# Two x loads of a decoder trunk's start change queue and place, and 18 idle matmuls stand where 14 stood

## The chip, the cores and the metric

One NeuronCore of a Trainium2 chip runs the whole program; the other cores are idle. The time is the device time of one launch in microseconds, the median over several runs. Inputs and weights lie in HBM, all in float32.

## The reference

Two layers of a decoder trunk on 256 tokens of width 2048. Layer 0 mixes with a retention group of four heads and a gated linear recurrence of eight channel blocks, layer 1 with block-sparse attention of sixteen heads; behind each mixer stands a gated MLP with a causal convolution of width 3. What the change touches is the very beginning, the norm and the first projection of layer 0:

```python
def rmsnorm(x, g):
    x32 = x.astype(jnp.float32)
    y = x32 * lax.rsqrt(jnp.mean(x32 * x32, axis=-1, keepdims=True) + EPS)
    return (y * g.astype(jnp.float32)).astype(x.dtype)
...
for l in range(DEPTH):
    hn = rmsnorm(x, norm_mix[l])
    if l % 2 == 0:
        y = even_mixer(hn, ...)      # proj = hn @ w_in, 2048 x 6144
    else:
        y = odd_mixer(hn, ...)
    x = x + y
    x = x + conv_ffn(rmsnorm(x, norm_ffn[l]), ...)
```

## The kernel before

**Layout.** x is held transposed in SBUF as `x_res`, 128 partitions by 16 k tiles by 256 tokens, and all weights stream through once. A matrix product is cut into output blocks of 512 columns (`NB`), and each block into eight chunks of two k tiles (`CT`), so a chunk of W is 256 rows by 512 columns, 512 KB. Chunks pass through a ring of four buffers (`RING`).

**The split.** Every float32 factor is split into a high and a low part of type float32r, which TensorE multiplies in three products. For W, ScalarE rounds `raw` to `w_hi` (line 368) and VectorE subtracts to get `w_lo` (line 942). For x, ScalarE makes `xs[..., 0, :]`, x times the norm's gain, rounded (line 397), and VectorE the remainder (line 991). The row scale of the norm is applied later, when a block is drained. TensorE then does per k tile and 128 output columns one matmul of w_hi with both parts of x (512 columns, line 663) and one of w_lo with the high part (256 columns, line 667); a chunk is eight of each.

**What sets the order.** There is no planner: each engine's program is written out by hand, and semaphores tie them together. Each engine walks the same sequence of chunks:

- SyncE (SP) issues the loads of W: chunk 0 is loaded as two tiles of 256 KB (line 286) with a semaphore of its own each, `tile_landed` and `landed[0]`. Between the following chunks it issues the x loads of k tiles 4 to 15 in three pieces of 512 KB (line 294), and a table of parameters (line 289). From the fifth chunk on, a load waits until VectorE has read the ring buffer (line 276).
- ScalarE issues at its start the gains of the norms (`par`, 32 KB, line 355) and two x loads of 256 KB, k tiles 0 and 1 (line 356, semaphore `first_loaded`) and k tiles 2 and 3 (line 357, `x_loaded[0]`). Then it loads a function table and rounds `ones`. For chunk 0 of the first block it waits for gains and first x load (lines 581 and 582), makes xs of two k tiles, waits for the first W tile, rounds it, waits for the second, rounds it. For chunk 1 it waits for `x_loaded[0]`, makes xs of k tiles 2 and 3, and rounds chunk 1 of W; then it squares the first four k tiles (line 392) for the norm's sum.
- VectorE follows with the low parts and, on odd chunks, sums the squares (lines 1001 to 1014), which end in `sumsq`.
- TensorE begins with `WARM` = 14 matmuls of a matrix of ones (lines 841 to 843), whose result nothing reads. They wait only for the memset of `ones` on GpSimd. Then come the chunks; ahead of chunk 2 stands a small product for the attention's bias, and ahead of chunk 7 the sum of squares over the partitions (line 712), which waits for `sumsq`.

A chunk of TensorE waits for `first_lo` (x's low part) and `lo_ready` (w_lo); in chunk 0 the first k tile waits for `tile_lo` alone.

Of the kernel before, what the change touches and what calls it, by code (L numbers as in the profile page):

```python
# [28 lines left out]
BT = NB // P  # L29
CT = 2  # L30
RING = 4
WARM = 14
KC = KT // CT
FC = FT // CT

# [91 lines left out]
def build(nc, x_t, params, w_gates, rope, decay, rel_bias, buckets, identity,  # L127
# [8 lines left out]
    def place(name, shape, dtype=F32, offset=None):  # L136
        size = int(np.prod(shape[1:])) * 4
        if offset is None:
            offset = at[0]
            at[0] += (size + 31) // 32 * 32  # L140
        return nc.alloc_sbuf_tensor_at(name, shape, dtype, offset=offset), offset
# [4 lines left out]
    x_res, _ = place("x_res", [P, KT, S])  # L146
# [61 lines left out]
    def sem(name):  # L208
        return nc.alloc_semaphore(name)
# [5 lines left out]
    first_loaded, gain_loaded = sem("first_loaded"), sem("gain_loaded")  # L215
    tile_landed, tile_hi, tile_lo, tail_done = sem("tile_landed"), sem("tile_hi"), sem("tile_lo"), sem("tail_done")
    x_loaded = [sem(f"x_loaded{j}") for j in range(4)]
# [50 lines left out]
    @block.sync  # L268
    def _(sp):
        def load(w, q, c, cols, rows):  # L270

            s = c % RING
            turn = q + c // RING
            if not (isinstance(turn, int) and turn == 0):

                sp.wait_ge(lo_ready, RING * (turn - 1) + s + 1)
            src = w[bass.ds(rows * (CT * P), CT * P), cols].rearrange("(t p) n -> p t n", p=P)
            sp.dma_start(raw[:, s, :, :], src).then_inc(landed[s], 16)

        for ph in phases:  # L280
            l = ph.layer
            for b, (_, _, col) in enumerate(ODD_BLOCKS if l else EVEN_BLOCKS):
                for c in range(KC):
                    if (l, b, c) == (0, 0, 0):
                        for u, landing in enumerate((tile_landed, landed[0])):
                            sp.dma_start(raw[:, 0, u, :], w_in[0][u * P:(u + 1) * P, col:col + NB]).then_inc(landing, 16)
                        continue
                    if (l, b, c) == (0, 0, 5):
                        sp.dma_start(par[:, 4 * KT:], params[:, 4 * KT:]).then_inc(const_loaded, 16)
                    load(w_in[l], ph.q_in + 2 * b, c, slice(col, col + NB), c)  # L290
                    if (l, b) == (0, 0) and c in (1, 3, 4):
                        j = (1, 3, 4).index(c) + 1
                        part = slice(j * BT, (j + 1) * BT)
                        sp.dma_start(x_res[:, part, :], x_t[:, part, :]).then_inc(x_loaded[j], 16)
            for b in range(OUTB):
                for c in range(KC):
                    load(w_out[l], ph.q_out + 2 * b, c, slice(b * NB, (b + 1) * NB), MIX_ORDER[l][c])
            with sp.Fori(0, PAIRS) as j:
                for half in range(2):
                    for c in range(KC):  # L300
                        load(w_up[l], ph.q_up + 4 * j + 2 * half, c, bass.ds(j * NB + half * D_FF, NB), c)
            for b in range(OUTB):
                cols = slice(b * NB, (b + 1) * NB)
                for c in DOWN_HEAD:
                    load(w_down[l], ph.q_down, FC * b + c, cols, c)
                with sp.Fori(*DOWN_TURNS) as t:
                    for i in range(RING):
                        load(w_down[l], ph.q_down + t, FC * b + i, cols, RING * t + i)
                for c in DOWN_TAIL:
                    load(w_down[l], ph.q_down, FC * b + c, cols, c)  # L310

        for m in range(BT):

            sp.wait_ge(last_added, m + 1)
            k = KT - BT + m
            sp.dma_start(out_t[:, k, :], x_res[:, k, :]).then_inc(last_stored, 16)
        sp.wait_ge(last_stored, 16 * BT)
# [33 lines left out]
    def _(eng):  # L351
# [1 line left out]
        step = Steps(eng, act_step)  # L353

        eng.dma_start(par[:, 0:4 * KT], params[:, 0:4 * KT]).then_inc(gain_loaded, 16)
        eng.dma_start(x_res[:, 0:CT, :], x_t[:, 0:CT, :]).then_inc(first_loaded, 16)
        eng.dma_start(x_res[:, CT:BT, :], x_t[:, CT:BT, :]).then_inc(x_loaded[0], 16)
        eng.wait_ge(consts_set, 1)
        act_f(ones_r[:, :], ones[:, :], ACT.Copy).then_inc(ones_rounded, 1)

# [33 lines left out]
        def split_x_pair(c):  # L394

            for t in range(CT * c, CT * (c + 1)):
                ins = act_f(xs[:, t, 0, :], x_res[:, t, :], ACT.Copy, scale=param("gain", t))
            ins.then_inc(first_hi, 1)
# [174 lines left out]
        for ph in phases:  # L573
            l = ph.layer
            post = odd_post if l else even_post
            for b in range(INB):
                if (l, b) == (0, 1):
                    eng.wait_ge(const_loaded, 16)
                for c in range(KC):
                    if (l, b, c) == (0, 0, 0):  # L580
                        eng.wait_ge(gain_loaded, 16)
                        eng.wait_ge(first_loaded, 16)
                        split_x_pair(0)
                        eng.wait_ge(tile_landed, 16)
                        act_f(w_hi[:, 0, 0, :], raw[:, 0, 0, :], ACT.Copy).then_inc(tile_hi, 1)
                        eng.wait_ge(landed[0], 16)
                        act_f(w_hi[:, 0, 1, :], raw[:, 0, 1, :], ACT.Copy).then_inc(hi_ready, 1)
                        continue
                    if (l, b) == (0, 0):

                        if c == 1 or c % 2 == 0:
                            eng.wait_ge(x_loaded[c // 2], 16)
                        split_x_pair(c)
                    split(ph.q_in + 2 * b, c)
                    if (l, b) == (0, 0) and c % 2:
                        square_x(c // 2, 0)
                    if b == 0 and l:
                        residual(c, 3, phases[0].n_down + 3, RING * ph.q_in, 1, 2)
                    if (l, b, c) == (0, 0, 5):
                        eng.wait_ge(line_done, 1)  # L600
                        act_f(line[0:HEADS, :], ps[0:HEADS, 5, 0:3 * P], ACT.Copy).then_inc(line_copied, 1)
                    if (l, b, c) == (0, 1, 4):
                        eng.wait_ge(lam_abs, 1)
                        act_f(small[:, 1, :], small[:, 0, :], ACT.Exp, scale=-1.0).then_inc(lam_exp, 1)
                    post(b, c)
                    if (b, c) == (1, 0):
                        stats(2 * l)
            for b in range(OUTB):
                for c in range(KC):
                    split(ph.q_out + 2 * b, c)  # L610
                    if b == 0:
                        post(INB, c)
                    else:
                        residual(c, b - 1, ph.n_out + b - 1, RING * (ph.q_out + 2 * b), (b - 1) % 2, 2 * l + 1)
            for c in range(KC):
                split(ph.q_up, c)
                residual(c, 3, ph.n_out + 3, RING * ph.q_up, 1, 2 * l + 1)
            for c in range(KC):
                split(ph.q_up + 2, c)
                if c == 0:  # L620
                    stats(2 * l + 1)
                mlp_post(c, ph, 0, 0)
            with eng.Fori(1, PAIRS) as j:
                for c in range(KC):
                    split(ph.q_up + 4 * j, c)
                    mlp_post(c, ph, 1, j - 1)
                for c in range(KC):
                    split(ph.q_up + 4 * j + 2, c)
                    mlp_post(c, ph, 0, j)
            for b in range(OUTB):  # L630
                for c in DOWN_HEAD:
                    split(ph.q_down, FC * b + c)
                    if b == 0:
                        mlp_post(c, ph, 1, PAIRS - 1)
                    else:
                        residual(c, b - 1, ph.n_down + b - 1, RING * ph.q_down + FC * b, (b - 1) % 2, None if l else 2)
                with eng.Fori(*DOWN_TURNS) as t:
                    for i in range(RING):
                        split(ph.q_down + t, FC * b + i)
                for c in DOWN_TAIL:  # L640
                    split(ph.q_down, FC * b + c)
# [3 lines left out]
    def _(pe):  # L645
# [195 lines left out]
        pe.wait_ge(consts_set, 1)  # L841
        for _ in range(WARM):
            mm(ps[:, 7, 0:P], ones[:, :], ones[:, :], start=True, stop=True)
# [656 lines left out]
```

## Time and profile before

| | us |
|---|---|
| median of 3 runs | 2256.04 (2255.95 to 2256.41) |
| the profiled execution | 2255.26 |
| its span, first to last instruction | 2253.5 |
| TensorE busy | 2245.5 |
| VectorE busy | 1544.1 |
| ScalarE busy | 1160.4 |
| granted clock of TensorE, mean | 1.00 |

The span is what the profile's rows measure from; the 1.8 us between it and the execution's own time lie around it. In the rows PE is TensorE, PEld its weight loads, ACT ScalarE, DVE VectorE, and SPq, ACTq and POOLq are the sequencers of SyncE, ScalarE and GpSimd, which issue DMAs. A DMA's "us to landing" counts from its issue to the semaphore that tells of its end. A float32 matmul of the idle kind shows as two rows.

### The profile page before, as it was taken

Reading aid. Unit: us, or ns where it says so; the run is one execution under the profiler, and the core shown is the slowest. Engines: PE = TensorE matmul, PEld = TensorE weight load, DVE = VectorE, ACT = ScalarE, POOL = GpSimd, SP = SyncE. Lnnn points to the kernel's source line nnn. Section 1 sums busy time; section 2 is a strip of 40 time slices with the busy share of each in tenths; the row PEclk is TensorE's granted clock in tenths of the full one; section 3 lists DMA queues with packets and bytes.
Section 4 is the critical chain, followed back from the end, with each engine's and each line's share of the span. In section 5 each row is a group of like instructions: output and inputs, shape, how many; then the busy total and the mean of one; then the engine's idle time right before and its main releaser. Section 6 shows DMA issues by size and latency. Waiting matters only on the chain.

```text
span 2253.5 us, 34392 instructions
## 1 busy us (share of the span) xinstructions
PE 2245.5 (100%) x12726; PEld 1954.2 (87%) x12726; DVE 1544.1 (69%) x1753; ACT 1160.4 (51%) x1342; POOL 7.2 (0%) x17
## 2 busy tenths in 40 slices
PE   9999999999999999999999999999999999999999
PEld 8888888888888888888888888888888888888888
DVE  7886776777777777554577777667777777774444
ACT  6654355555555555444355555555555555553333
POOL 0000000000000000000000000000000000000000
PEclk9999999999999999999999999999999999999999
DMA  8555555666566656566665554556666666566664
GB/s 273 181 178 166 189 177 187 181 193 192 181 189 188 200 177 194 189 183 191 199 212 165 171 178 158 168 185 183 191 191 184 187 187 201 179 190 204 198 188 144
DMA packets 216386, 420.92 MB, mean 187 GB/s; under 512 B 13061, under 2 KB 13589, under 8 KB 216176
## 3 DMA queue, kind: packets, MB, share of 16 engines
q1 hardware_dynamic: 214416, 413.59, 59.1%
q0 software_dynamic: 1456, 5.65, 0.7%
q8 instruction: 56, 0.92, 0.2%
q10 hardware_dynamic: 432, 0.56, 0.1%
q14 instruction: 26, 0.21, 0.0%
HBM read 417.62 MB, written 2.12 MB: 186 GB/s over the span
## 4 chain that ended last, share of the span: by engine, by line
PE 99%; DMA 0%; DVE 0%; ACT 0%; ACTq 0%; issue 0%
PE ps L663 61%; PE ps L667 30%; PE ps L704 2%; PE ps L705 2%; PE ps L706 2%; PE ps L743 0%; PE ps L789 0%; DMA x_res<-x_t 0%; PE ps L801 0%; PE ps L725 0%; PE ps L744 0%; PE ps L737 0%; PE ps L800 0%; DVE aq L950 0%; PE ps L761 0%; ACT cross L376 0%
## 5 line engine op out<-in xcount | busy, mean ns | idle before, releaser
L942 DVE TENSOR_TENSOR w_lo<-raw,w_hi 128x1024 fp32r<-128x1024 f32 x783 | 948.5, 1223 | 497.7 <-ACT w_hi L368 478.1
L663 PE MATMUL ps<-xs,w_hi 128*128 128x512 f32 x3968 | 1248.3, 396 | 3.6 <-DVE w_lo L1378 3.1
L368 ACT ACTIVATE w_hi<-raw 128x1024 fp32r<-128x1024 f32 x783 | 811.4, 1055 | 561.3 <-PE ps L667 506.8
L667 PEld LDWEIGHTS ps<-xs,w_lo 128*128 128x128 f32 x3968 | 745.4, 188 | 176.1
L667 PE MATMUL ps<-xs,w_lo 128*128 128x256 f32 x3968 | 779.6, 278 | 0.0
L663 PEld LDWEIGHTS ps<-xs,w_hi 128*128 128x128 f32 x3968 | 605.0, 189 | 6.2 <-DVE xs L991 3.3
L663 PE MATMUL ps<-act,w_hi 128*128 128x512 f32 (+1 forms) x1912 | 600.7, 395 | 0.0
L667 PEld LDWEIGHTS ps<-act,w_lo 128*128 128x128 f32 x1912 | 359.2, 188 | 84.9
L667 PE MATMUL ps<-act,w_lo 128*128 128x256 f32 (+1 forms) x1912 | 375.6, 278 | 0.0
L663 PEld LDWEIGHTS ps<-act,w_hi 128*128 128x128 f32 x1912 | 291.1, 189 | 0.4 <-DVE av L967 0.4
L379 ACT ACTIVATE cross<-ps 128x1024 f32<-128x1024 f32 x72 | 74.0, 1027 | 119.2 <-PE ps L667 118.8
L958 DVE TENSOR_TENSOR h<-ps,cross 128x1024 f32<-128x1024 f32 x52 | 63.6, 1224 | 75.3 <-ACT cross L379 75.3
L704 PE MATMUL ps<-w_hi,xs 128*128 128x512 f32 x192 | 74.8, 389 | 0.0
L705 PE MATMUL ps<-w_lo,xs 128*128 128x512 f32 x192 | 74.8, 389 | 0.0
L706 PE MATMUL ps<-w_hi,xs 128*128 128x512 f32 x192 | 74.7, 389 | 0.0
L422 ACT ACTIVATE buf_g<-h,par 128x256 f32<-128x256 f32 x88 | 45.8, 591 | 43.3 <-DVE h L960 43.3
L960 DVE TENSOR_TENSOR h<-h,rstd 128x1024 f32<-128x1024 f32 x54 | 66.2, 1225 | 2.0
L422 ACT ACTIVATE buf_v<-h,par 128x256 f32<-128x256 f32 x88 | 45.8, 591 | 40.4 <-DVE h L960 40.4
L426 ACT ACTIVATE buf_g<-buf_g 128x1024 f32<-128x1024 f32 x22 | 23.4, 1062 | 66.7 <-DVE buf_g L1060 66.7
L430 ACT ACTIVATE act<-buf_v 128x1024 f32 (+1 forms) x22 | 23.4, 1063 | 63.7 <-DVE buf_v L1070 63.7
L706 PEld LDWEIGHTS ps<-w_hi,xs 128*128 128x128 f32 x192 | 36.0, 188 | 7.6
L704 PEld LDWEIGHTS ps<-w_hi,xs 128*128 128x128 f32 x192 | 36.0, 188 | 7.4
(186 smaller groups left out, 864.6 us busy)
## 6 DMA issues: line engine op xcount, KB each, us to landing
raw<-w_up SPq DMA_DIRECT2D x352, 512.0 KB, 3.7
raw<-w_in SPq DMA_DIRECT2D x191, 512.0 KB, 3.9
raw<-w_down SPq DMA_DIRECT2D x176, 512.0 KB, 4.6
raw<-w_out SPq DMA_DIRECT2D x64, 512.0 KB, 4.7
bias<-bias_line POOLq DMA_DIRECT2D x1, 2048.0 KB, 11.6
x_res<-x_t SPq DMA_DIRECT2D x3, 512.0 KB, 7.7
out_t<-x_res POOLq DMA_DIRECT2D x3, 512.0 KB, 3.2
gates_w<-w_gates POOLq DMA_DIRECT2D x1, 1024.0 KB, 5.4
```

The costliest lines, as they stand in the source:

```text
L368: act_f(w_hi[:, s, :, :], raw[:, s, :, :], ACT.Copy).then_inc(hi_ready, 1)
L379: act_f(cross[:, :, :], ps[:, 4 * group:4 * group + 4, S:2 * S], ACT.Copy).then_inc(cross_copied, 1)
L422: ins = act_f(buf[:, t, :], h[:, t, :], ACT.Identity, scale=w, bias=b)
L426: act_f(buf_g[:, :, :], buf_g[:, :, :], ACT.Gelu_apprx_tanh).then_inc(gelu_done, 1)
L663: return mm(ps[:, 4 * group + m, :], w_hi[:, s, u, m * P:(m + 1) * P], rhs, start=first and u == 0, stop=False)
L667: return mm(ps[:, 4 * group + m, 0:S], w_lo[:, s, u, m * P:(m + 1) * P], rhs[:, 0:S], start=False, stop=last and u == CT - 1)
L704: mm(out, x_hi, w_hi[:, s, u, :], start=first and u == 0, stop=False)
L705: mm(out, x_hi, w_lo[:, s, u, :], start=False, stop=False)
L706: ins = mm(out, x_lo, w_hi[:, s, u, :], start=False, stop=last and u == CT - 1)
L942: tt(w_lo[:, s, :, :], raw[:, s, :, :], w_hi[:, s, :, :].bitcast(F32), ALU.subtract).then_inc(lo_ready, 1)
L958: tt(dst, ps[:, 4 * group:4 * group + 4, 0:S], cross[:, :, :], ALU.add).then_inc(acc_drained, 1)
L960: tt(dst, dst, spread(rstd[:, 0:S], BT), ALU.mult).then_inc(normed, 1)
```

## The change

1. The x load of k tiles 0 and 1 (`first_loaded`) is issued by SyncE as its first DMA, ahead of the W tiles, in place of ScalarE.
2. The x load of k tiles 2 and 3 (`x_loaded[0]`) stays on ScalarE, but is issued only once `gain_loaded` and `first_loaded` have been waited for, right ahead of the first xs.
3. `WARM` is 18 in place of 14.

```diff
@@ -29,7 +29,7 @@
-WARM = 14
+WARM = 18
@@ -282,6 +282,7 @@ sync
                     if (l, b, c) == (0, 0, 0):
+                        sp.dma_start(x_res[:, 0:CT, :], x_t[:, 0:CT, :]).then_inc(first_loaded, 16)
                         for u, landing in enumerate((tile_landed, landed[0])):
                             sp.dma_start(raw[:, 0, u, :], w_in[0][u * P:(u + 1) * P, col:col + NB]).then_inc(landing, 16)
                         continue
@@ -353,8 +354,6 @@ scalar
         eng.dma_start(par[:, 0:4 * KT], params[:, 0:4 * KT]).then_inc(gain_loaded, 16)
-        eng.dma_start(x_res[:, 0:CT, :], x_t[:, 0:CT, :]).then_inc(first_loaded, 16)
-        eng.dma_start(x_res[:, CT:BT, :], x_t[:, CT:BT, :]).then_inc(x_loaded[0], 16)
         eng.wait_ge(consts_set, 1)
@@ -580,6 +579,7 @@ scalar
                         eng.wait_ge(gain_loaded, 16)
                         eng.wait_ge(first_loaded, 16)
+                        eng.dma_start(x_res[:, CT:BT, :], x_t[:, CT:BT, :]).then_inc(x_loaded[0], 16)
                         split_x_pair(0)
```

The start of ScalarE's program before, with what each instruction waits for (`consts_set` is the memset of ones, `landed1` chunk 1 of W):

```order
L355 DMA par<-params 128x64
L356 DMA x_res<-x_t 128x512
L357 DMA x_res<-x_t 128x512
L359 ACT_TABLE_LOAD
L359 ACTIVATE ones_r<-ones 128x128 [waits consts_set]
L397 ACTIVATE xs<-x_res,par 128x256 [waits first_loaded,gain_loaded]
```

The same place in the changed kernel, whose lines there are numbered one less:

```order
L356 DMA par<-params 128x64
L358 ACT_TABLE_LOAD
L358 ACTIVATE ones_r<-ones 128x128 [waits consts_set]
L582 DMA x_res<-x_t 128x512 [waits first_loaded,gain_loaded]
L396 ACTIVATE xs<-x_res,par 128x256 x2
```

One x load is gone from ScalarE's program, and the other has moved behind the wait for gains and first x load, which it now carries; the first xs follows it.

The start of SyncE's program in the changed kernel (`raw` is the ring of W, `x_res` x, `par` the parameters):

```order
L285 DMA x_res<-x_t 128x512
L287 DMA raw<-w_in 128x512 x2
L278 DMA raw<-w_in 128x2x512
L295 DMA x_res<-x_t 128x1024
L278 DMA raw<-w_in 128x2x512 x2
```

The first of these rows is new; before, the program began with the two W tiles, and the rest is in the old order.

## Rows read from the trace of the kernel before

**Rows 1.** The page: busy time, share of the span and instructions of each engine.

```profile
PE 2245.5 (100%) x12726; PEld 1954.2 (87%) x12726; DVE 1544.1 (69%) x1753; ACT 1160.4 (51%) x1342; POOL 7.2 (0%) x17
```

**Rows 2.** Stretches (us): TensorE's busy time (x instructions), granted clock, DMA share, GB/s.

```profile
31.00:1130.00 1099.00, 1099.00 (x6256) 1.00 0.61 188
1130.00:2253.50 1123.50, 1119.77 (x6324) 1.00 0.59 183
```

**Rows 3.** The chain that ended last, 0 to 40 us: start, us, what.

```profile
1.68 7.13 DMA x_res<-x_t
...
8.83 0.91 ACT xs L397 x2
...
12.10 0.69 PE ps L663 x2
```

**Rows 4.** Timeline, 1 to 12 us: start, us, engine, line, operation, [idle before].

```profile
1.20 0.45 ACTq L356 DMA_DIRECT2D x_res<-x_t  x1
...
6.22 0.91 ACT L397 ACTIVATE xs<-x_res,par 128x256 fp32r<-128x256 f32 x2 [2.46 <-DMA x_res<-x_t]
7.04 0.61 ACT L585 ACTIVATE w_hi<-raw 128x512 fp32r<-128x512 f32 x1
...
8.88 0.70 PE L663 MATMUL ps<-xs,w_hi 128*128 128x512 f32 x2 [3.12 <-DVE w_lo L1378]
...
11.52 0.40 PE L667 MATMUL ps<-xs,w_lo 128*128 128x256 f32 x2
```

**Rows 5.** DMA issues at 0.76, 1.2, 1.67, 2.14 and 9.77 us: KB, us to landing.

```profile
raw<-w_in SPq DMA_DIRECT2D x1, 256.0 KB, 3.5
par<-params ACTq DMA_DIRECT2D x1, 32.0 KB, 3.7
...
raw<-w_in SPq DMA_DIRECT2D x1, 256.0 KB, 4.7
x_res<-x_t ACTq DMA_DIRECT2D x1, 256.0 KB, 4.9
...
raw<-w_in SPq DMA_DIRECT2D x1, 512.0 KB, 7.2
...
x_res<-x_t SPq DMA_DIRECT2D x1, 512.0 KB, 7.7
...
x_res<-x_t SPq DMA_DIRECT2D x1, 512.0 KB, 6.7
```

**Rows 6.** DMA queues (q1 SP's, q10 ScalarE's), 6.5 to 7 us, then 8 to 9 us.

```profile
q1 hardware_dynamic: 47, 0.09, 49.9%
q10 hardware_dynamic: 39, 0.07, 46.5%
...
q10 hardware_dynamic: 2, 0.00, 0.7%
```

**Rows 7.** Stretches of the start, with the columns of the second group.

```profile
2.00:3.30 1.30, 1.30 (x8) 1.00 0.88 206
2.00:5.10 3.10, 3.10 (x22) 1.00 0.95 256
9.00:11.00 2.00, 2.00 (x12) 1.00 1.06 395
```

**Rows 8.** Timeline, 11.5 to 30 us: third xs, then towards the sums of squares.

```profile
11.55 0.89 ACT L397 ACTIVATE xs<-x_res,par 128x256 fp32r<-128x256 f32 x2
...
18.87 1.07 ACT L368 ACTIVATE w_hi<-raw 128x1024 fp32r<-128x1024 f32 x1 [0.24 <-DMA raw<-w_in]
...
20.48 1.22 DVE L942 TENSOR_TENSOR w_lo<-raw,w_hi 128x1024 fp32r<-128x1024 f32 x1
...
28.97 0.43 DVE L1014 TENSOR_TENSOR sumsq<-sumsq,h 128x256 f32<-128x256 f32 x1
...
29.72 0.30 PEld L712 LDWEIGHTS ps<-sumsq,ones 128*128 128x128 f32 x2
```

**Rows 9.** The idle matmuls from 4.2 to 5.8 us: ns min/median/max, first and last start.

```profile
L843 PE MATMUL ps<-ones x14: 275/275/275, 4.0 to 5.5; 128*128 128x128 f32 x14
```

## The prediction

> **What bounds the kernel now.** I read the page first, then TensorE's busy time by stretches, then the chain in order of time, then the timeline and the DMA issues of the first 30 us. TensorE is busy 2245.5 of 2253.5 us [rows 1], 8.0 us short. From 31 us to 1130 us it is never idle, and from there to the end it is idle 3.7 us [rows 2]. So 4.3 us lie in the first 31 us, and 3.12 of them between the idle matmuls and the first real one [rows 4]. That is all the change touches: two x loads move, and the idle matmuls grow in number.
>
> The chain in order of time says whether that wait counts [rows 3]. It doesn't run through it. It follows the second x load (k tiles 2 and 3) from its issue at 1.68 to 8.81, then the two xs activations of chunk 1 at 8.83, and by w_hi and w_lo of chunk 1 reaches TensorE at 12.10. So the start of chunk 0 at 8.88 has slack: its products end at 11.92, and TensorE stands still for 0.18 us before chunk 1 [rows 3, 4]. **The number that moves the end is when chunk 1 can start, 12.10 us, not when chunk 0 starts.**
>
> What chunk 0 waits for: the first x load was issued at 1.20 and took 4.9 us (6.1), xs followed at 6.22, and TensorE at 8.88, that is 2.66 us behind xs [rows 4, 5]. The parameters land at 0.75 + 3.7 = 4.45, the first W tile at 0.76 + 3.5 = 4.26, the second at about 1.19 + 4.7 = 5.9, chunk 1's W at 1.67 + 7.2 = 8.87 [rows 5].
>
> **The change part by part.**
>
> *The first x load goes to the front of SP's queue.* It is now the first transfer there, issued at 0.76 on an idle machine, and of the size of the W tile that stood there: I take its 3.5 us, so it lands at 4.26 in place of 6.1. The parameters stay on ScalarE's queue and land at 4.45, so they now release ScalarE, at about 4.5.
>
> *The second x load is issued there, behind both waits and ahead of xs.* Its issue occupies ScalarE's sequencer for 0.45 us [rows 4], and it now lies on the path of chunk 0: xs starts at about 5.0. Behind the waiting issue stands everything that ScalarE does: xs, w_hi. With the same 2.66 us from xs, chunk 0 starts at 5.0 + 2.66 = 7.66, which is 1.2 us earlier than before, and its 3.05 us end at 10.7.
>
> *Three loads are moved past on SP's queue.* The W tiles and chunk 1's W go out one issue (0.45 us) later and stand behind 256 KB more. W tile 0 is wanted at 5.0 + 0.82 = 5.82 (w_hi of a tile, at 7.04, stands 0.82 behind xs, at 6.22 [rows 4]). It now has the second place, whose transfer landed at 5.9 while ScalarE's queue took its share; that share is now free until the second x load starts. I cost it at nothing, at worst 0.1. W tile 1, in third place, is wanted at 6.3; it is bounded by 5.9 from below and by the 8.87 of what held the bytes behind it from above. At 8.87 it would be 0.6 us dearer than before in chunk 1, since w_hi of tile 1 (0.61 us) stands ahead of the xs of chunk 1: 8.87 + 0.61 = 9.48 against 8.83. Over all queues 206 GB/s moved from 2.0 to 3.3 us, 0.27 MB, about the first load with the parameters, and that load landed at 4.26, 1.0 us later; to 5.1 us it is 256 GB/s for 3.1 us, 0.79 MB, about three loads with the parameters [rows 7], so with the same lag tile 1 lands at 6.1. I take that: just in time. Chunk 1's W has the same bytes ahead of it in both kernels once the second x load is served (1.6 MB over both queues), so I leave it at 8.87. The third x load has slack: it landed at 2.14 + 7.7 = 9.8 and was wanted at 11.55 [rows 5, 8].
>
> *When the second x load lands decides the gain.* Before: issued 1.68, queued behind the first one, landed 8.81. Now: issued at 4.5 on an empty queue of its own. Bounds for its duration: 3.5 us (first on a queue that was empty) and 4.9 us (behind 32 KB of small packets); further off lies 6.7 us, for 512 KB on SP's queue at 9.77 [rows 5]. With both queues full they shared the engines evenly (49.9% against 46.5%), and its last packets straggled: 2 of them moved after 8.0 us [rows 6]. I take 3.8 us, near the row for an empty queue with a little for the fuller neighbour: 8.3 us. The Trainium skill, page "DMA: Bandwidth & Descriptors", section "Queues, rings and completion order", says that each DMA engine takes turns between the queues it has work for, packet by packet. That speaks against moving x into W's queue, since a queue of its own has a turn of its own; the even shares agree with it, and by it the first x load gains only because it stands at the front. The same page ("Anatomy of one DMA") fits 2.0 us plus the bytes at 436 GB/s, an estimate of 2.6 us here, by which x would land at 7.1 and chunk 1's W would decide, for a gain of 0.8 us; every load of this stretch took longer than the fit.
>
> So xs of chunk 1 starts at about 8.35 in place of 8.83, w_hi 0.82 behind it at 9.17 in place of 9.65 (its W is there at 8.87), and chunk 1 on TensorE at 11.6 in place of 12.10. **Gain 0.5 us.** Chunk 0 ends at 10.7, so a new wait of 0.9 us stands before chunk 1: most of what chunk 0 gains is given back there.
>
> *Does the 0.5 us survive?* VectorE comes to the sums of squares at 28.97 + 0.43 = 29.40, and TensorE wants them at 29.72: 0.32 us of slack. On the way ScalarE's w_hi of chunk 5 waited for its W until 18.87, and VectorE's w_lo behind it started at 20.48, 0.54 us after w_hi was done at 19.94 [rows 8]. The DMA engines are saturated up to there (395 GB/s at 9 to 11 us [rows 7]), so that W can't come earlier; VectorE can be 0.5 us earlier and no more. TensorE could gain at most 0.54 + 0.32 = 0.9 us before the sums of squares take over as the wait. The forecast of 0.5 fits within it.
>
> *18 idle matmuls in place of 14.* Their late rows start 14 in 1.5 us [rows 9], 0.11 each; four matmuls are eight rows, 0.9 us. They end at 5.76 + 0.9 = 6.65, before 7.66, and nothing waits for them. The granted clock of 9 to 11 us, behind the old gap of 3.1 us, is 1.00 (2.4 GHz) [rows 7]. So they cost and bring nothing. Their cover is the wait for x: gone only if chunk 0 could start before 6.65.
>
> **Sum.** The profiled execution took 2255.26 us (span 2253.5); less 0.5 it is 2254.8. The median of the runs shown is 2256.04, 0.78 above the profiled one, so I forecast 2256.04 - 0.5 = 2255.5 us. A measurement can't tell 0.2% (4.5 us) from no change, so by that bound this is the same time.
>
> **The rivals.**
> - *Both loads come early.* x lands by 8.0 or sooner and chunk 1's W sooner than 8.87. Then w_hi of chunk 1 starts at 8.87 or before and the gain runs into the cap of 0.9 us: 2255.1. For it: the queue is empty. Against: the stragglers.
> - *The second x load is late (slower).* It is the first thing that chunk 1 needs, and the change lets it wait for the landing of another load. From 4.3 us of duration on (8.81 - 4.5) chunk 1 starts later than before. With 4.9 us it lands at 9.4, 0.6 us late: 2256.6. With 6.7 it is 2.4 us late: 2258.4. For it: the same 256 KB took 4.9 from issue when the queues were less full. To cost over 0.2% it would have to take 8.8 us, more than the 7.1 of the load that was queued behind another.
> - *The clock.* The Trainium skill, page "TensorE: Matmul & The Clock Gate", Part 1, says that an idle TensorE falls back to half clock. If that happened in the timed runs but not in the profiled one, chunk 0 ran at half pace, up to 2.9 us longer (3.05 less the 0.18 that was waited anyway), and the smaller gap (6.65 to 7.66) gives it back: 2253.1. The trace speaks against it: the granted clock is 1.00 behind the gap.
> - *The change doesn't bring the x load forward* (the first place on SP's queue lands no sooner than 6.1): then the second is issued at 6.2 and lands at 10 or so, 1.2 us late: 2257.2. Against: the first place landed at 4.26.
>
> **How the numbers follow.** Forecast 0.5, both early 0.2, late x 0.24, clock 0.03, not brought forward 0.03. Every one of them lies within 4.5 us of the old median, so the same time has 0.97; 0.015 on each side is for a wait further back that no row shows. The range takes in a gain of 1 us and a loss of 0.6 to 1, with the 0.5 to 0.8 us by which single executions differ here: 2254.2 to 2257.2.
>
> **What would show it.** In the changed kernel's trace: first x load landed near 4.3, ScalarE's xs at 5.0, first real matmul at 7.7, second x load landed near 8.3, second chunk at 11.6 behind a wait of about 0.9 us for w_lo, VectorE's last sum at 28.9 and no wait of TensorE for it, idle matmuls over at 6.65. It would be wrong if chunk 1 started after 12.1, or if a wait stood after 31 us that wasn't there before.

## The result, and the profile after

| | before | after |
|---|---|---|
| median | 2256.15 us (22 runs, 2254.72 to 2257.79) | 2259.47 us (22 runs, 2258.38 to 2260.58) |
| the profiled execution, its span | 2255.26, 2253.5 | 2259.08, 2257.3 |

The changed kernel is slower by 3.3 us: the ratio of the times is 1.0016, with a 95% interval of 1.0010 to 1.0022. The direction is clear, though the size lies below the 0.2% that the prediction took as its bound. The span grew by 3.8 us in the profiled executions, and all of it lies at the front.

TensorE's waits in the changed kernel (us in total, times, longest), which answer to the two in [rows 3, 4]:

```profile
PE ps L663 <- DVE w_lo L942: 3.8, 1, 3.8
...
PE ps L663 <- DVE w_lo L1378: 0.2, 1, 0.2
```

The wait before chunk 0 shrank from 3.12 to 0.2 us, and a wait of 3.8 us for w_lo of a later chunk stands where 0.18 us stood. The chain that ended last, in order of time, answers to [rows 3]:

```profile
0.75 3.78 DMA par<-params
...
4.55 6.53 DMA x_res<-x_t
...
11.11 0.91 ACT xs L396 x2
...
12.99 1.24 DVE w_lo L942
...
14.37 0.70 PE ps L663 x2
```

It still runs through the second x load. That load is issued at 4.55, behind the parameters' landing, and takes 6.53 us, so chunk 1 starts at 14.37 and not at 12.10. The timeline of the same stretch (start, us, engine, line, operation, [idle before]), against [rows 4]:

```profile
4.55 0.33 ACTq L582 DMA_DIRECT2D x_res<-x_t  x1
4.93 0.91 ACT L396 ACTIVATE xs<-x_res,par 128x256 fp32r<-128x256 f32 x2 [2.13 <-DMA par<-params]
...
6.27 0.61 ACT L587 ACTIVATE w_hi<-raw 128x512 fp32r<-128x512 f32 x1
...
7.59 0.70 PE L663 MATMUL ps<-xs,w_hi 128*128 128x512 f32 x2 [0.21 <-DVE w_lo L1378]
...
14.37 0.70 PE L663 MATMUL ps<-xs,w_hi 128*128 128x512 f32 x2 [3.75 <-DVE w_lo L942]
...
15.98 1.05 PE L663 MATMUL ps<-xs,w_hi 128*128 128x512 f32 x2
...
19.60 0.74 PE L663 MATMUL ps<-xs,w_hi 128*128 128x512 f32 x2
```

Up to chunk 0 all goes as forecast: xs at 4.93, both W tiles in time, the first real matmul at 7.59 where it was at 8.88. The last two matmul rows show a second loss. A pair of w_hi matmuls took 1.05 us at 15.98, against 0.70 for the pair at 14.37. The stretches of TensorE (busy time, granted clock, DMA share, GB/s), against [rows 2, 7]:

```profile
14.37:15.60 1.23, 1.23 (x6) 1.00 1.01 405
15.60:19.60 4.00, 4.00 (x14) 0.57 0.82 275
19.60:22.50 2.90, 2.90 (x17) 1.00 0.68 218
35.00:1134.00 1099.00, 1099.00 (x6255) 1.00 0.61 188
1134.00:2257.30 1123.30, 1119.62 (x6323) 1.00 0.59 183
```

Behind the 3.75 us in which TensorE stood still, the clock fell from 2.4 GHz to 1.2 GHz for most of four microseconds (granted clock 0.57 on average). From chunk 1 to chunk 2 it is 5.23 us (14.37 to 19.60), where before it was 3.70 (12.10 to 15.80, with the bias product in both): 1.53 us lost to the clock. With the 2.27 us by which chunk 1 starts later that is 3.80 us, the whole growth of the span. From 35 us on nothing changed: no idle time up to 1134 us, and 3.7 us from there to the end.

Where did the load spend its 6.53 us? The DMA issues at 0.76, 1.68, 2.14 and 4.55 us (KB, us to landing), against [rows 5]:

```profile
x_res<-x_t SPq DMA_DIRECT2D x1, 256.0 KB, 3.6
par<-params ACTq DMA_DIRECT2D x1, 32.0 KB, 3.8
...
raw<-w_in SPq DMA_DIRECT2D x1, 256.0 KB, 4.1
...
raw<-w_in SPq DMA_DIRECT2D x1, 512.0 KB, 5.3
...
x_res<-x_t ACTq DMA_DIRECT2D x1, 256.0 KB, 6.5
```

And the DMA queues' packets, MB and share of the engines, first from 5 to 8 us and then from 8 to 9, against [rows 6]:

```profile
q1 hardware_dynamic: 450, 1.12, 101.3%
...
q1 hardware_dynamic: 125, 0.25, 72.7%
q10 hardware_dynamic: 54, 0.11, 30.4%
```

From 5 to 8 us no packet of ScalarE's queue (q10) moved at all, though its load was issued at 4.55. SP's queue kept the engines busy at 101%. The load's first packet moved at 8.2 us, 3.7 us after the issue, and only from there do both queues move together. So more than half of the load's 6.53 us went by before it shared anything; it stood in line.

### The profile page after: what moved, and what is told of

The parts are those of the page before. It is cut to its first block, busy times and chain, and to the rows that moved or that the text cites. A ratio compares the mean times of both kernels' runs of the same rounds, so it can differ in the third digit from the quotient of the medians.

```text
span 2257.3 us, 34408 instructions
## 1 busy us (share of the span) xinstructions
PE 2248.6 (100%) x12734; PEld 1956.9 (87%) x12734; DVE 1544.2 (68%) x1753; ACT 1160.3 (51%) x1342; POOL 7.3 (0%) x17
## 4 chain that ended last, share of the span: by engine, by line
PE 99%; DMA 0%; DVE 0%; ACT 0%; issue 0%
PE ps L663 61%; PE ps L667 30%; PE ps L704 2%; PE ps L705 2%; PE ps L706 2%; PE ps L743 0%; PE ps L789 0%; PE ps L801 0%; PE ps L725 0%; DMA x_res<-x_t 0%; PE ps L744 0%; PE ps L737 0%; DMA par<-params 0%; PE ps L800 0%; DVE aq L950 0%; PE ps L761 0%
```

## The experiments

Several theories of the loss stood open. **Theory A:** the DMA engines work through what is already outstanding before they turn to a load issued later, whatever queue it comes by, as if all issues stood in one line. What counts is the second load's place in time among SP's issues. **The others:** moving the first load did the harm (B); a load issued this late on ScalarE's queue takes 6.5 us whatever stands ahead (C); the idle matmuls or the clock made the loss.

| label | what | median us | before, same chip | us against it |
|---|---|---|---|---|
| e1 | first load moved, nothing else | 2254.03 | 2256.01 | -2.0 |
| e2 | second load waits, nothing else | 2260.55 | 2256.01 | +4.5 |
| e3 | 18 idle matmuls, nothing else | 2255.52 | 2256.01 | -0.5 |
| e4 | the change with 14 idle matmuls | 2259.67 | 2256.01 | +3.7 |
| e5 | the change, gap filled | 2258.21 | 2255.83 | +2.4 |
| e7 | the change, SP holds from W of chunk 3 | 2259.70 | 2255.83 | +3.9 |
| e8 | all on SP's queue | 2254.89 | 2255.83 | -0.9 |
| e9 | second load by GpSimd | 2259.86 | 2256.05 | +3.8 |
| e11 | e1, second load issued behind `ones_r` | 2254.02 | 2256.05 | -2.0 |
| e12 | e1 with 18 idle matmuls | 2253.96 | 2256.05 | -2.1 |

Each median is over 10 or 11 runs. The intervals of the ratio are about 0.0009 wide to either side (2 us), so e1 alone (0.9992, 0.9983 to 1.0001) is just not clear of no change; e1, e11 and e12 give the same time in three kernels, and all 11 times of e12 (up to 2254.28) lie below the lowest of the 27 of the kernel before on the same chip (2254.36). For steps under 1 us the traces' start times are the better measure. e6 and e10 have a single time each (2257.86 and 2258.27) and serve for their traces.

### One part at a time: e1, e2, e3, e4

e1, from the kernel before:

```diff
                     if (l, b, c) == (0, 0, 0):
+                        sp.dma_start(x_res[:, 0:CT, :], x_t[:, 0:CT, :]).then_inc(first_loaded, 16)
...
-        eng.dma_start(x_res[:, 0:CT, :], x_t[:, 0:CT, :]).then_inc(first_loaded, 16)
         eng.dma_start(x_res[:, CT:BT, :], x_t[:, CT:BT, :]).then_inc(x_loaded[0], 16)
```

> The kernel before with one part of the change alone: the first x load goes to the front of SP's queue, the second stays on ScalarE's queue and is issued at once, at about 1.2 us. The trace of the changed kernel shows its second x load issued at 4.55 and no packet of ScalarE's queue before 8.0. Theory A (one line): what SP and ScalarE issue is served from one line in the order of issue, so a late issue stands behind all that SP has put there. Then here the second x load has only 0.25 to 0.5 MB ahead of it and lands by about 6.5, chunk 0 starts at 7.2 (4.45 + 0.05 + 2.66), and chunk 1 is bound by its W (landed 8.87 before, about 7.5 to 9 now): at 10.5 to 11.5 in place of 12.1, a gain of 0.6 to 1.5 us over the kernel before. Theory B (moving the first load itself does harm, since it pushes W back): chunk 1 starts at 12.1 or later and the time is that of before or above.

Timeline of e1, with the issue of the second load and what led to chunk 1:

```profile
1.20 0.45 ACTq L357 DMA_DIRECT2D x_res<-x_t  x1
...
6.53 0.63 ACT L587 ACTIVATE w_hi<-raw 128x512 fp32r<-128x512 f32 x1 [0.41 <-DMA raw<-w_in]
...
7.07 0.90 ACT L397 ACTIVATE xs<-x_res,par 128x256 fp32r<-128x256 f32 x2
...
10.37 0.70 PE L663 MATMUL ps<-xs,w_hi 128*128 128x512 f32 x2 [0.26 <-DVE w_lo L942]
```

The second load, issued at 1.20, landed 4.5 us later at 5.7, before ScalarE had even rounded the second W tile (6.53), so that nothing waited for it. Chunk 1 started at 10.37 in place of 12.10, and the time fell by 2.0 us, both a little better than theory A's 10.5 to 11.5 and 0.6 to 1.5 us. The first part of the change is good; theory B falls.

e2, from the kernel before:

```diff
-        eng.dma_start(x_res[:, CT:BT, :], x_t[:, CT:BT, :]).then_inc(x_loaded[0], 16)
...
                         eng.wait_ge(first_loaded, 16)
+                        eng.dma_start(x_res[:, CT:BT, :], x_t[:, CT:BT, :]).then_inc(x_loaded[0], 16)
```

> The kernel before with the other part alone: both x loads on ScalarE's queue, the second issued behind the waits for gains and first load, so at about 6.2. Theory A (one line): it stands behind everything that SP issued up to 4.9 us (3.1 MB), of which the deepest is served at about 12 us, so it lands at 11 to 12.5, chunk 1 starts at 14.4 to 15.6, and the kernel is 2 to 5 us slower than before (half clock in the gap behind chunk 0 included). Theory B (the harm is in moving the first load): it lands some 3.5 to 4.5 us after its issue, at 10, and the loss is about 1.2 us.

```profile
6.09 0.33 ACTq L582 DMA_DIRECT2D x_res<-x_t  x1
...
9.12 1.19 PE L663 MATMUL ps<-xs,w_hi 128*128 128x512 f32 x2 [2.62 <-DVE w_lo L1378]
...
12.61 0.91 ACT L396 ACTIVATE xs<-x_res,par 128x256 fp32r<-128x256 f32 x2 [4.19 <-DMA x_res<-x_t]
...
15.87 1.19 PE L663 MATMUL ps<-xs,w_hi 128*128 128x512 f32 x2 [2.27 <-DVE w_lo L942]
```

The timeline of e2 shows the load issued at 6.09 and ScalarE's xs behind it at 12.61: 6.5 us again, 1.5 us later than in the changed kernel because it was issued 1.5 us later. Chunk 1 starts at 15.87, at half clock (1.19 us for a pair), and the kernel is 4.5 us slower, within the 2 to 5 us that theory A gave, though chunk 1 starts a little later than its 14.4 to 15.6. From chunk 1 to chunk 2 it is 5.19 us here (15.87 to 21.06), so the half clock is part of this loss too. The second part alone does the harm, and more of it than in the changed kernel, where the first part takes some back.

e3 is one line, `WARM = 18`, in the kernel before.

> The kernel before with 18 idle matmuls. Expected 2256.1, no difference (within 0.3 us): they end at about 6.65 to 7.4, before the first tile at 8.88. If the idle matmuls cost something by themselves, the start of chunk 0 moves later than 8.88.

2255.52 against 2256.01 is within what the runs can tell: no difference shown. Chunk 0 did start later in its trace, at 9.42, but the idle matmuls were over at 7.09 there; it was the first x load that took 5.5 us in that execution in place of 4.9, and the end didn't follow.

e4 is the changed kernel with `WARM = 14`.

> The changed kernel with 14 idle matmuls. If the number doesn't matter: as the changed kernel, 2259.5, chunk 1 at about 14.4, and a stretch at half clock behind the wait for chunk 1. If the 18 matter for the clock: the clock falls earlier or for longer, and it is 0.5 to 1.5 us slower than 2259.5.

2259.67, as with 18. The clock did fall earlier, as these stretches show (granted clock in the column behind the busy time), but was back earlier too:

```profile
14.30:15.50 1.20, 1.20 (x4) 0.50 1.02 408
15.50:19.50 4.00, 4.00 (x17) 0.78 0.89 304
```

So 14 or 18 idle matmuls at the start make no difference that the runs show, in either kernel.

### The clock by itself: e5

The changed kernel, with the gap between chunk 0 and chunk 1 filled:

```diff
                         chunk_products(ph.q_in + 2 * b, c, xs, CT * c, group, c == 0, c == KC - 1, drained,
                                        tile_lo if (l, b, c) == (0, 0, 0) else None)
+                    if (l, b, c) == (0, 0, 0):
+                        for _ in range(14):
+                            mm(ps[:, 7, 0:P], ones[:, :], ones[:, :], start=True, stop=True)
```

> The changed kernel with 14 more idle matmuls between chunk 0 and chunk 1, in the gap of 3.75 us. Theory: 2.3 us of the loss are the later landing of the second x load and 1.5 us are the half clock behind the gap. Then chunk 1 still starts at about 14.4, the granted clock stays at 1.00 behind it, chunk 2 starts at 18.1 in place of 19.6, and the time is 1.5 us under that of the changed kernel: 2258.0. If the clock is no part of it: 2259.5 or more.

Timeline of e5's TensorE with the fill, the start of chunk 1 and of chunk 2, and the granted clock of that stretch:

```profile
10.17 3.29 PE L880 MATMUL ps<-ones 128*128 128x128 f32 x28
14.07 0.70 PE L663 MATMUL ps<-xs,w_hi 128*128 128x512 f32 x2 [0.61 <-DVE w_lo L945]
...
17.77 0.72 PE L663 MATMUL ps<-xs,w_hi 128*128 128x512 f32 x2
...
14.07:18.00 3.93, 3.93 (x19) 1.00 0.92 333
```

With the fill the granted clock stays at 1.00, and from chunk 1 to chunk 2 it is 3.70 us again (14.07 to 17.77), exactly that of the kernel before. The time fell from 2259.5 to 2258.2, or from 3.3 to 2.4 us above the kernel before if each is taken against its own runs of it; the intervals of the two (1.0010 to 1.0022 and 1.0003 to 1.0021) overlap, so the times alone don't settle it. The traces do: in e5 chunk 1 starts 1.97 us later than before and the span is 2.0 us longer (2255.5 against 2253.5), with nothing left for the clock. The rest of the loss is the load.

### What the load waits for: e6, e10, e7, e9, e8, e11

e6, e10 and e7 are the changed kernel with one wait of SP more, `sp.wait_ge(x_loaded[0], 16)`, at three places: ahead of the third x load (e6), of W of chunk 2 (e10), of W of chunk 3 (e7). The piece shown is e10's; e7 has `(0, 0, 3)`. They differ in how many bytes SP has issued before the second x load is: 1.3, 1.8 and 2.4 MB, and 2.9 or more in the changed kernel, where one more issue was under way at 4.55.

```diff
+                    if (l, b, c) == (0, 0, 2):
+                        sp.wait_ge(x_loaded[0], 16)
                     load(w_in[l], ph.q_in + 2 * b, c, slice(col, col + NB), c)
```

> The changed kernel, with SP issuing nothing behind W of chunk 1 until the second x load has landed. Theory A (one line for both queues, order of issue): 1.3 MB stand ahead in place of 2.9, most of it moved when the second load is issued at 4.55, so ScalarE's queue has its first packet near 6 and the load lands at 7.5 to 8.3. Rival C (a load issued this late on ScalarE's queue takes 6.5 us whatever stands ahead): it lands at 11. Later chunks will wait for x and W, which were held, so the whole time is no measure here.

> The changed kernel with SP holding back W of chunk 2 and what follows until the second x load has landed; 1.8 MB are issued ahead, 1.3 MB of them outstanding at 4.3 us. If up to 1.4 MB outstanding go first: first packet when nearly all 1.3 MB are moved, at 7.3 to 7.8, landing at 9 to 10.5. If it were the count of issued DMAs and not the bytes that decides, it would be midway between 8.6 (hold from chunk 1's x on) and 11.1.

> The changed kernel, with SP holding back only W of chunk 3 and what follows. Theory A: 2.4 MB stand ahead in place of 2.9 to 3.4; in the changed kernel the first packet came when 0.9 to 1.4 MB of what stood ahead was still to be moved, so here it comes at 5.3 to 6.6 and the load lands at 8.4 to 9.7, between the two others. Chunk 1 starts 3.3 us behind the landing, at 11.7 to 13.0, and the time is 2256 to 2257.5. Rival C: it lands at 11, as in the changed kernel.

For each, the load's row (KB, us to landing), and ScalarE's queue in the microsecond in which it first moved (packets, MB, share): e6 from 6 to 7 us,

```profile
x_res<-x_t ACTq DMA_DIRECT2D x1, 256.0 KB, 4.5
...
q10 hardware_dynamic: 110, 0.21, 55.0%
```

e10 from 7 to 8 us,

```profile
x_res<-x_t ACTq DMA_DIRECT2D x1, 256.0 KB, 6.1
...
q10 hardware_dynamic: 68, 0.14, 36.4%
```

and e7 from 7 to 8 us, with hardly any packets:

```profile
x_res<-x_t ACTq DMA_DIRECT2D x1, 256.0 KB, 6.9
...
q10 hardware_dynamic: 12, 0.02, 6.3%
```

The first packets of the load, from narrower windows of the same view, and what SP's queue moved between the issue and that packet:

| | issued | SP's MB issued by then | first packet at | us after the issue | SP's MB moved in between | us to landing |
|---|---|---|---|---|---|---|
| e1 | 1.20 | 0.3 | 3.2 | 2.0 | 0.2 | 4.5 |
| e6 | 4.12 | 1.3 | 6.0 | 1.9 | 0.6 | 4.5 |
| e10 | 4.21 | 1.8 | 7.3 | 3.1 | 1.0 | 6.1 |
| e7 | 4.23 | 2.4 | 7.7 | 3.5 | 1.2 | 6.9 |
| changed kernel | 4.55 | 2.9 | 8.2 | 3.7 | 1.4 | 6.5 |
| e2 | 6.09 | 3.1 | 9.8 | 3.7 | 1.4 | 6.5 |

Theory C falls with e6: a load issued just as late takes 4.5 us when little stands ahead (it landed at 8.6, just past theory A's 7.5 to 8.3). With more ahead the first packet comes later, as e10 shows. e7 is a miss of mine: I had it land at 8.4 to 9.7, and it landed at 11.1, no sooner than in the changed kernel. The delay doesn't grow with all that SP has issued; it levels off. So a late load goes behind what is outstanding, up to some 1.2 to 1.4 MB, and then shares the engines with what is left. In its strict form theory A is wrong as well: when the load's first packet moved, 0.5 MB of what SP had issued before it still stood unmoved in e7 and 0.8 MB in the changed kernel. Why the wait ends there is open. No run tells bytes from the number of issues or of packets: e10 landed at 10.3, within the 9 to 10.5 expected by bytes and near the 9.9 expected by the count of issues.

Holding SP back is no cure. In e10 and e7 chunk 1 starts at 13.6 and 14.4. In e6 it starts at 11.87, but TensorE then waits for later chunks that were held, and its one time is 2257.86.

e9 takes the second load off ScalarE and gives it to GpSimd, behind the same two waits:

```diff
+        pool.wait_ge(gain_loaded, 16)
+        pool.wait_ge(first_loaded, 16)
+        pool.dma_start(x_res[:, CT:BT, :], x_t[:, CT:BT, :]).then_inc(x_loaded[0], 16)
```

> The changed kernel with the second x load issued by GpSimd, behind the same two waits, in place of ScalarE. So far: of ScalarE's queue the first packet came 3.8 to 4.2 us after the issue where SP had over 1.4 MB outstanding, and SP's queue moved 1.3 to 1.5 MB in between; with 0.8 MB outstanding it came after 2.1 us. If that line is one of the two queues that SP and ScalarE issue to: the load lands by 9, chunk 1 starts by 12.3, and the time is 2257.3 or less. If it is in the DMA engines themselves, whatever the queue: it lands at 11 or later, and the time is 2259.5.

The load's row in e9, and GpSimd's queue (q0) from 8 to 9 us, where its 4 KB packets begin:

```profile
x_res<-x_t POOLq DMA_DIRECT2D x1, 256.0 KB, 6.5
...
q0 software_dynamic: 16, 0.07, 16.6%
```

Issued at 4.57, first of these packets at 8.6, 6.5 us to landing, as by ScalarE. The wait (4.0 us to the first packet) is no shorter by this queue. The expectation gives the earlier delays as 3.8 to 4.2 us and 2.1 us; by the first packets, as in the table, they are 3.5 to 3.7 us and 1.9 us.

e8 is the changed kernel with the second load on SP's queue behind the two W tiles (`sp.dma_start(...)` behind the loop over the tiles, none on ScalarE).

> The changed kernel with the second x load on SP's queue too, right behind the two W tiles, and no wait ahead of it. Theory A: it lands at about 6.3 and W of chunk 1 at about 8, chunk 1 starts at 10.4 to 10.8, and the time is that of the kernel with the first load moved alone, 2254.0. If the second load needs a queue of its own: chunk 1 starts later than 11, and the time is above 2255.

```profile
6.58 0.91 ACT L397 ACTIVATE xs<-x_res,par 128x256 fp32r<-128x256 f32 x2 [0.43 <-DMA x_res<-x_t]
8.72 1.06 ACT L368 ACTIVATE w_hi<-raw 128x1024 fp32r<-128x1024 f32 x1 [1.23 <-DMA raw<-w_in]
```

ScalarE's timeline in e8: the second x load lands in time for xs at 6.58, but now ScalarE waits 1.23 us for W of chunk 1, until 8.72, which in e1 it could round from 7.90. That load of W goes out at 2.62 here, behind the second x load, and at 2.14 in e1. Chunk 1 starts at 11.18, past the 10.4 to 10.8 of the one expectation and the 11 of the other, yet ahead of the 12.10 of before. The time, 2254.89, lies between e1 and the kernel before and is clear of neither.

e11 is e1 with the second load's issue moved behind the rounding of `ones_r`.

> The kernel with the first x load alone moved, and the second issued on ScalarE behind the rounding of ones, with no wait for a load. If the sequencer issues it at about 1.7 us, ahead of most of SP's issues: as the kernel with the first load moved alone, 2254.0. If it is issued at about 2.8, with 1.3 to 1.8 MB of SP's outstanding: it lands at 8.5 to 9.5, chunk 1 starts at 11.8 to 12.8, and the time is 2255.5 to 2257. Either way the place among SP's issues decides, and not the wait as such.

ScalarE's sequencer issued it at 1.27, since it hands an activation on without waiting for its end. That is as early as in e1, and the time is the same, 2254.02. It therefore tells nothing of a late issue, but shows that the line of code is harmless as long as no wait for a load stands ahead.

### A version that beats both: e12

> The first x load at the front of SP's queue, the second issued at once on ScalarE, and 18 idle matmuls. If the idle matmuls are over before the first tile is ready: as with 14, 2254.0. If their first part runs at half clock for as long as in the last kernels (28 rows took up to 6.2 us), 36 rows end near 7.1 to 7.5, at or just past the 7.1 of the first tile, and it costs 0 to 0.3 us. Against the kernel before it is 1.7 to 2 us faster, which repeats the gain of the first part alone.

The first and third part of the change without the second: 2253.96 us, 2.1 under the kernel before and 5.4 under the changed one (each taken against its own runs of the kernel before). Chunk 1 starts at 10.53. Its idle matmuls ended at 7.22, just as chunk 0 began, so no room was left ahead of it. With e1 at 2254.03, 14 or 18 idle matmuls are the same here too, and the simplest best version is e1.

## Why the prediction was wrong

It forecast 2255.5 in a range of 2254.2 to 2257.2; the kernel takes 2259.5. In the traces chunk 1 starts 2.27 us later and not 0.5 earlier, and the clock, for which the sum had nothing, takes 1.53 us more.

- **The place of the bound: right.** The end hung on chunk 1 and the second x load, not on chunk 0, in both kernels. Chunk 0 gained 1.29 us (1.2 forecast), and none of it reached the end.
- **The first load and chunk 0: right.** Landed 0.76 + 3.6 (3.5 forecast), xs at 4.93 (5.0), first real matmul at 7.59 (7.66). The W tiles came in time.
- **W of chunk 1: off, without effect.** I left it at 8.87; it landed at 2.14 + 5.3 = 7.4. That nothing of the second load moved until then is only part of the reason: in e1, where that load moved from 3.2 us on, it landed at 2.14 + 5.7 = 7.8.
- **The step that failed: "I take 3.8 us, near the row for an empty queue".** It took 6.53. The row I chose was a load issued when the whole machine was idle; at 4.55 only its own queue was empty. The argument leaned on [rows 6], where two queues share evenly, and read it as the right of a queue to its turn at once. Those rows only show packets that had long been issued. The experiments put in its place: behind a deep enough backlog of another queue (from e7's 2.4 MB issued ahead on, of which 0.6 had moved) a load has its first packet only 3.5 to 3.7 us after its issue from ScalarE's queue, and 4.0 us from GpSimd's. With 3.8 us for the load chunk 1 would have started at 11.6; it started at 14.37. The Trainium skill's rule that the engines take turns between queues ("DMA: Bandwidth & Descriptors", section "Queues, rings and completion order") agrees with the stretch behind 8.2 us, where both queues move (56.9% against 44.9% from 9 to 10 us), but not with the three microseconds before. The same page's fit of 2.0 us plus the bytes ("Anatomy of one DMA"), an estimate of 2.6 us here, stands there for DMAs that GpSimd issues; GpSimd's load in e9 took 6.5 us.
- **The rival with the other sign: right in kind and in size, too low in chance.** "The second x load is late" gave 6.7 us and chunk 1 2.4 us late; measured 6.5 and 2.27. The 6.7 us row (a load issued into a full SP queue) was the one nearest in kind, and I treated it as further off. It had 0.24, with a time of 2256.6 at 4.9 us, and the range ended at 2257.2, short of the 2258.4 that the rival itself gave for 6.7 us. The 1.1 us between 2258.4 and the measured time is less than the clock's share.
- **The clock: a term put at nothing.** I looked for the clock only in the gap before chunk 0, as a gain. The new gap before chunk 1, which I put at 0.9 us, became 3.75 us, and the clock fell behind it, for another 1.53 us. That the extra idle matmuls cost and bring nothing was right (e3, e4, e12), with less room than I thought: they ended at 7.38 and not at 6.65, 0.21 us ahead of chunk 0.
- **Late or not, nothing further back moved.** The sums of squares were ready in time, and behind 35 us the two traces agree.

The idle matmuls of the changed kernel, against [rows 9]:

```profile
1.01 6.37 PE L843 MATMUL ps<-ones 128*128 128x128 f32 x36 [1.01 <-POOL ones L323]
```

36 rows took 6.37 us, where I had added 0.9 us to 4.75. The slow pace of the start (421 ns a row, against 275 later) lasted to about 5 us in this execution and to about 4 us in the one before the change (the granted clock of [rows 7] reads 1.00 there all the same), and it varies from one to the next: 28 rows took 4.75 us before and 5.49, 5.86 and 6.24 us in e2, e1 and e4, so an estimate from one trace has that much play.

## What to carry to other kernels

A small load that something waits for is best issued before the bulk transfers, not merely on a queue of its own: in these runs a queue's emptiness said nothing about how soon its load moved, since the DMA engines had so much outstanding from another. When a load is made to wait for another, look at how many bytes the other issuers will have put out by then, and price it from a row that was issued into the same backlog. And when a wait on TensorE is moved rather than removed, price the new gap's length against the clock as well: here the wait cost 2.3 us and the clock behind it 1.5.

## What the runs showed of the hardware that was not expected

- A load of 256 KB took 4.5 us when issued at 4.12 us with 1.3 MB issued ahead, and 6.5 to 6.9 us with 2.4 to 3.1 MB ahead, from ScalarE's queue and from GpSimd's alike. Between issue and first packet SP's queue moved no more than 1.4 MB.
- TensorE's granted clock didn't follow the length of the gap alone. It was at 1.00 behind 3.12 us of standing still (before), and in e2 chunk 0 started at half pace (1.19 us for a pair) behind 2.62 us. Behind 3.75 us in the changed kernel it fell only after the first 1.2 us of work had run at full pace.
- ScalarE's sequencer issued a DMA at 1.27 that stands in the program behind a table load and an activation which ran only from 2.50 to 2.81 us (e11).
